# Fourteen chunks of an input projection in pairs by Strassen's method, with the weight sums on GpSimd

## The chip, the core and the metric

The kernel runs on one core of one Trainium2 chip. The metric is the device time of one execution in microseconds (us), and less is better.

## The reference

Two layers of an encoder on 256 tokens of width 2048, in float32. A layer normalises x, multiplies it by one wide matrix (`w_in`), and feeds the columns of the product to three mixers: latent attention (MLA, 8 heads), dilated attention (12 heads) and mLSTM (4 heads). Their outputs pass `w_out` and are added to x. Then comes a mixture of 16 experts, of which each token uses 2.

```python
xn = rms_norm(x, norm_mix[l])
c_q, c_kv, k_rope, dq, dk, dv, mu, mv, mo, mg = jnp.split(xn @ w_in[l], split_at, axis=-1)
...
x = x + jnp.concatenate([y_mla, y_dil, y_ml], axis=-1) @ w_out[l]
x = x + hier_moe(rms_norm(x, norm_ffn[l]), ...)
```

The change touches only `xn @ w_in[l]`, and of it the columns of dq, dk, dv, mv and mo: 3840 columns, that is 15 chunks of 256.

## The kernel before, in words

Every engine has its own program, written out by hand, and they meet at semaphores. All weights come from HBM through one queue (SyncE, the rows "SPq") into a ring of six slots of 2 MB (`ring`) and, for the experts, into three more places (XN, PR and BIAS, once their own data is no longer needed). `plan_slots` gives each load its slot, and a load is issued when the last reader of the load before it in that slot has finished. `plan_banks` gives each TensorE result its PSUM bank: `freed(name)` waits until the last result in that bank has been read, `ready(name)` until the result is there, `copied(name)` until it has been read.

A layer runs as follows. XN is x times its gain (not yet divided by its norm). First come three small chunks (c0 to c2: the latents), then the chunks mu0, mu1, mu2 of the mLSTM, with the up-projection of the latents between mu1 and mu2, and the gate rows after mu2 (`rows0`, `rows1`). During this VectorE (DVE) does the rotary embedding and the norms of the MLA queries and keys, ending with the signal `a_n`, and reads the banks of mu0 to mu2 (`keep_u`).

Then comes the stage that the change is about: chunks m0 to m14. `main(j, t)` computes 128 tokens (t is 0 or 1) by 256 columns of chunk j as 16 matmuls, one for each 128 rows of the weight: the stationary operand is a 128x128 block of XN, the moving one 128x256 of the chunk's slot. A chunk is thus 32 matmuls into one PSUM bank, two token halves side by side, and it is read from the bank once, by ScalarE (ACT, even j) or DVE (odd j), into PR, with the factor 1/norm. Chunks take banks 1 and 0 in turn, m0 bank 1.

Between the halves stand the attention steps. `MLA_AT` puts the seven steps of the MLA attention behind half 4, 6, ... 16, `DIL_AT` the nine steps of the dilated one behind halves 20 to 28, and `CONV_AT` the five taps of the mLSTM's convolution, which only DVE does, behind halves 3, 5, 7, 9 and 11. A step is a software pipeline: TensorE does the values of head pair s-3, the scores of pair s-1 and the transposes of pair s-2; DVE takes the maxima, scales the probabilities (`prob`) and reads transposes back; ScalarE does the exponentials. DVE works strictly in the order of its program.

After m14 come the output projection with the mLSTM between its parts, the router, and the experts, two at a time. GpSimd (POOL) only issues a few transfers.

Of the kernel before, what the change touches and what calls it, by code (L numbers as in the profile page):

```python
# [20 lines left out]
F32 = mybir.dt.float32  # L21
I32 = mybir.dt.int32
ALU = mybir.AluOpType
# [79 lines left out]

K_ID, K_FLIP, K_MASK = 0, P, 2 * P
# [70 lines left out]
def plan_banks():  # L175
# [17 lines left out]
    for j in range(3 * W_D // CH):  # L193
        b.once(f"m{j}", (j + 1) % 2)
        if j == 0:
            b.once("gcols", 2)
        for t in range(NT):
            if NT * j + t in MLA_AT:
                plan_attention(b, "a", H_A // 2, MLA_AT[NT * j + t])
    for j in range(3 * W_D // CH, N_SEQ):  # L200
        b.once(f"m{j}", (j + 1) % 2)
        for t in range(NT):
            at = NT * j + t - NT * (3 * W_D // CH)
            if at in DIL_AT:
                plan_attention(b, "d", H_D // 2, DIL_AT[at])
# [43 lines left out]

def plan_attention(b, k, pairs, s):  # L250
# [36 lines left out]
EXPERT_SLOTS = (IN_BIAS, 5, 0, 1, 2, 3, 4, IN_XN, IN_PR)  # L287


def plan_slots():  # L290
# [3 lines left out]
    at, held = NSLOT - 1, None  # L294
    for name in FRONT:
        if at % NSLOT == held:
            at += 1
        r.once(name, at % NSLOT)
        if name == "mw":
            held = at % NSLOT  # L300
        at += 1
    for j, name in enumerate(EXPERT):
        r.once(name, EXPERT_SLOTS[j % len(EXPERT_SLOTS)])
# [10 lines left out]
LAST_READER.update({f"B{i}": f"ob{(TILES * (i + 1) - 1) // (KT - K_A)}" for i in range(N_OUT * (KT - K_A) // TILES)})  # L314
LAST_READER.update({f"{n}{j}_{i}": f"{n}_{i}" for n in ("g0", "u0", "g1", "u1") for j in range(2) for i in range(NE // 2)})
# [19 lines left out]
def build(nc, a, consts, onehot, lncount, out):  # L335
    with ExitStack() as ctx:
# [3 lines left out]
        def sem(name):  # L340
# [37 lines left out]
            sem, ("sweep_load", "sweep_pe", "sweep_act", "sweep_dve", "sweep_own"))  # L378
        bias_dram = nc.dram_tensor("bias_dram", (H_D, 2 * S), F32).ap()
# [87 lines left out]
        par_in, small_in = sem("par_in"), sem("small_in")  # L467
        x_in, const_in, bias_in, bias_out, pos_in, rw_in, done = map(
# [16 lines left out]
        for name, n in (("sq", 4), ("sq_sum", 1), ("xg_even", KT // 2), ("xg_odd", KT // 2), ("rstd_x", 1), ("lat_std", 1), ("lat_n", 1),  # L485
# [32 lines left out]
        def empty(name, l):  # L518
# [4 lines left out]
            before = order[at - 1]  # L523
            if at > 0:
# [10 lines left out]


# [81 lines left out]
        def _(pool):  # L618
# [13 lines left out]
            for l in range(DEPTH - 1):  # L632
# [7 lines left out]
        def _(pe):  # L640
# [156 lines left out]
            for l in range(DEPTH):  # L797
# [28 lines left out]
                for t in range(NT):  # L826
                    for j in range(4):
# [9 lines left out]
                        last.then_inc(*made(name))  # L837
                project_u(2, l)
# [15 lines left out]
                for j in range(3 * W_D // CH):  # L854
                    for t in range(NT):
                        main(j, t)
                        if j == 0 and t == NT - 1:

                            pe.wait_ge(*freed("gcols", l))
                            for d in range(2):  # L860
                                pe.wait_ge(*after("rows_ready", l, d))
                                for n in range(2):
                                    for u in range(NT):
                                        c = ((n * 2 + d) * NT + u) * H_M
                                        last = mm(bank("gcols")[:, c:c + H_M], grow(d, (2, 4)[n])[:, u * P:(u + 1) * P], K[0:H_M, 0:H_M])
                            last.then_inc(*made("gcols"))
                        if NT * j + t in MLA_AT:
                            s = MLA_AT[NT * j + t]
                            if s == 0:
                                pe.wait_ge(*after("a_n", l))  # L870
                            attention("a", H_A // 2, s, l)
                for j in range(3 * W_D // CH, N_SEQ):
                    for t in range(NT):
                        main(j, t)
                        at = NT * j + t - NT * (3 * W_D // CH)
                        if at in DIL_AT:
                            if DIL_AT[at] == 0:
                                pe.wait_ge(*after("d_n", l))
                            attention("d", H_D // 2, DIL_AT[at], l)
# [4 lines left out]
                for j in range(N_OUT):  # L884
                    for q in range(2):
                        project_out("a", j, q, l)
                        if 2 * j + q in MLSTM_AT:
                            h = MLSTM_AT[2 * j + q]
                            if h == 1:
                                pe.wait_ge(*after("v_ones", l))  # L890
                                for c in range(N_SEQ - 6, N_SEQ - 3):
                                    pe.wait_ge(*copied(f"m{c}", l))
# [218 lines left out]

        qv, kv = t_h(q_mla, H_A), t_h(k_mla, H_A)
# [8 lines left out]
        def _(dve):  # L1121
# [121 lines left out]
            for l in range(DEPTH):  # L1243
# [22 lines left out]
                def keep_u(m):  # L1266
                    dve.wait_ge(*ready(f"mu{m}", l))
                    for b in range(2):
                        ins = dve.tensor_tensor(u_raw(2 * m + b), bank(f"mu{m}")[:, b * S:(b + 1) * S], rstd_b[:, 0:S], ALU.mult)
# [35 lines left out]
                keep_u(1)  # L1305
                for t in range(NT):
                    for j in (2, 3):
# [6 lines left out]
                                        src[:, :, NOPE:]).then_inc(*read(name))  # L1314

# [45 lines left out]
                for j in range(3 * W_D // CH):  # L1361
                    for t in range(NT):
                        at = NT * j + t
                        if t == NT - 1 and j % 2:
                            keep(f"m{j}", l, DQ + j * CH, CH)
                        if t == NT - 1 and j in (2, 5):
                            squares_of(j // 3)
                        if t == NT - 1 and j == 5:
                            dve.wait_ge(*after("d_std", l))
                            do(dve.reciprocal(rstd_d[:, :, :, :], std_d[:, :, :, :]))  # L1370
                            do(dve.tensor_scalar(rstd_d[:, 0, :, :], rstd_d[:, 0, :, :], HD_D ** -0.5, None, ALU.mult))
                            for n, lo in enumerate((DQ, DK)):
                                w = t_h(PR[:, :, lo:lo + W_D], H_D)
                                ins = dve.tensor_tensor(w, w, rstd_d[:, n, :, :].unsqueeze(3).to_broadcast([P, NT, H_D, HD_D]), ALU.mult)
                                if n == 0:
                                    own.did(ins)
                                else:
                                    ins.then_inc(*signal("d_n"))
                        if j == 1 and t == 0:
                            dve.wait_ge(*ready("gcols", l))  # L1380
                            dve.tensor_copy(gcol[:, :, :, :, :].rearrange("p n d t h -> p (n d t h)"), bank("gcols")[:, 0:32]).then_inc(*read("gcols"))
                        if at in MLA_AT:
                            attention("a", H_A // 2, MLA_AT[at], l)
                        if at in CONV_AT:
# [579 lines left out]
```

## Time and profile before

| | us |
|---|---|
| median of three runs (1984.39 to 1989.51) | 1985.12 |
| the profiled execution | 1986.55 |
| its span, first to last instruction | 1984.9 |
| TensorE busy in the span | 1929.6 |
| DVE / ACT / POOL busy | 472.4 / 317.6 / 5.8 |

In the rows of the profile below, PE is a TensorE matmul, "ps" is PSUM, and each float32 matmul of 256 columns appears as two records, so "x64" is 32 matmuls of the program. PEclk is the granted TensorE clock as a share of 2.4 GHz: 1.00 is the upper of its two levels, 0.50 the lower one.

### The profile page before, as it was taken

How to read it: one execution, taken by the hardware profiler on the slowest of the kernel's cores; microseconds unless marked ns; L12 is line 12 of the kernel's file. 1: busy time of each engine (PE TensorE's matmuls, PEld its weight loads, DVE VectorE, ACT ScalarE, POOL GpSimd, SP SyncE). 2: the span in 40 equal slices, each digit the busy share in tenths (PEclk: the TensorE clock that was granted, in tenths of full speed). 3: DMA queues.
4: the chain of work that ended last, by engine and by line, in shares of the span. 5: the costliest groups of instructions: out<-in, count | busy, mean ns of one | idle time of the engine just before them, and what ended most of it. 6: DMA issues, size and time to landing. Idle time of an engine off the chain costs nothing.

```text
span 1984.9 us, 26562 instructions
## 1 busy us (share of the span) xinstructions
PE 1929.6 (97%) x11730; PEld 1457.5 (73%) x11730; DVE 472.4 (24%) x1233; ACT 317.6 (16%) x831; POOL 5.8 (0%) x12
## 2 busy tenths in 40 slices
PE   6999999999899999999899999999998999999998
PEld 6788888788766666656597888877887666666665
DVE  2233313122211111221133232222222012110212
ACT  2122122210211110111021221222102111110110
POOL 0000000000000000000000000000000000000000
PEclk9999999999899999999999999999998999999999
DMA  8353333223599999999963433322346999999995
GB/s 330 137 209 127 128 127 127 92 106 149 212 414 427 428 426 427 428 427 427 413 238 146 151 116 137 130 88 88 128 157 255 426 426 427 426 428 426 428 427 242
DMA packets 39831, 538.39 MB, mean 271 GB/s; under 512 B 4665, under 2 KB 4793, under 8 KB 7201
## 3 DMA queue, kind: packets, MB, share of 16 engines
q1 hardware_dynamic: 38160, 531.46, 65.3%
q0 software_dynamic: 1296, 5.13, 0.7%
q8 instruction: 97, 1.59, 0.3%
q14 instruction: 22, 0.17, 0.0%
q10 hardware_dynamic: 256, 0.04, 0.0%
HBM read 534.49 MB, written 2.12 MB: 270 GB/s over the span
## 4 chain that ended last, share of the span: by engine, by line
PE 97%; issue 1%; DVE 1%; DMA 1%; ACT 0%; SPq 0%; DVEq 0%
PE ps L642 94%; PE ps L693 1%; DMA ring<-in_w_lat 1%; PE ps L986 0%; PE ps L709 0%; PE ps L701 0%; PE ps L907 0%; PE ps L1026 0%; ACT PR L1849 0%; PE ps L780 0%; ACT L1862 0%; SPq L562 0%; DVE v_mla L1565 0%; PE ps L820 0%; DVE prob L1607 0%
## 5 line engine op out<-in xcount | busy, mean ns | idle before, releaser
L642 PE MATMUL ps<-ring,scr 128*64 128x256 f32 (+2 forms) x3520 | 562.7, 428 | 7.1 <-issue 7.1
L642 PE MATMUL ps<-ring,XN 128*128 128x256 f32 (+2 forms) x2304 | 484.6, 371 | 17.1 <-DMA ring<-in_w_lat 17.1
L642 PEld LDWEIGHTS ps<-ring,XN 128*128 128x128 f32 x2304 | 424.5, 191 | 66.9 <-issue 19.1
L642 PEld LDWEIGHTS ps<-ring,scr 128*64 128x64 f32 (+1 forms) x3520 | 319.8, 139 | 203.9 <-issue 113.2
L642 PE MATMUL ps<-XN,ring 128*128 128x256 f32 x768 | 170.4, 381 | 0.9 <-DVE prob L1155 0.9
L642 PE MATMUL ps<-BIAS,scr 128*64 128x256 f32 (+1 forms) x608 | 159.3, 420 | 6.9 <-issue 6.9
L642 PEld LDWEIGHTS ps<-XN,ring 128*128 128x128 f32 x768 | 144.7, 190 | 26.6 <-issue 7.7
L642 PE MATMUL ps<-PR,scr 128*64 128x256 f32 (+2 forms) x576 | 158.3, 430 | 0.7 <-DVE scr L1600 0.7
L642 PE MATMUL ps<-PR,ring 128*128 128x256 f32 x640 | 142.9, 383 | 0.0
L642 PE MATMUL ps<-XN,scr 128*64 128x256 f32 (+1 forms) x576 | 141.6, 403 | 0.3 <-issue 0.2
L642 PEld LDWEIGHTS ps<-PR,ring 128*128 128x128 f32 x640 | 121.9, 192 | 19.1 <-issue 2.7
L642 PE MATMUL ps<-v_mla,PR 128*128 128x128 f32 x1024 | 122.7, 283 | 4.1 <-DVE v_mla L1565 4.1
L642 PEld LDWEIGHTS ps<-v_mla,PR 128*128 128x128 f32 x1024 | 121.2, 200 | 4.2 <-issue 4.2
L642 PE MATMUL ps<-PR,prob 128*128 128x256 f32 x512 | 118.7, 386 | 5.0 <-issue 3.8
L1589 DVE TENSOR_TENSOR v_mla<-scr,ps 128x256 f32<-128x256 f32 x32 | 13.5, 421 | 429.8 <-PE ps L642 429.8
L642 PEld LDWEIGHTS ps<-PR,prob 128*128 128x128 f32 x512 | 96.0, 192 | 24.2 <-issue 12.1
L642 PEld LDWEIGHTS ps<-BIAS,scr 128*64 128x64 f32 x608 | 83.6, 139 | 34.2 <-issue 9.9
L642 PEld LDWEIGHTS ps<-PR,scr 128*64 128x64 f32 (+1 forms) x576 | 81.2, 146 | 34.6 <-issue 24.9
L642 PEld LDWEIGHTS ps<-XN,scr 128*64 128x64 f32 x576 | 78.3, 137 | 29.4 <-issue 19.5
L1874 ACT ACTIVATE scr<-ps,par 128x128 f32<-128x128 f32 x240 | 63.8, 412 | 222.7 <-PE ps L642 222.7
L1578 DVE TENSOR_TENSOR X<-X,ps 128x512 f32<-128x512 f32 x128 | 87.9, 687 | 31.9 <-PE ps L642 31.0
L1882 ACT ACTIVATE scr<-ps 128x256 f32<-128x256 f32 x32 | 12.3, 383 | 378.7 <-PE ps L642 378.7
(231 smaller groups left out, 1009.7 us busy)
## 6 DMA issues: line engine op xcount, KB each, us to landing
ring<-in_moe_w_up SPq DMA_DIRECT2D x44, 2048.0 KB, 22.7
ring<-in_moe_w_down SPq DMA_DIRECT2D x44, 2048.0 KB, 26.5
ring<-in_moe_w_gate SPq DMA_DIRECT2D x42, 2048.0 KB, 24.5
ring<-in_w_main SPq DMA_DIRECT2D x36, 2048.0 KB, 8.1
ring<-in_w_out_a SPq DMA_DIRECT2D x10, 2048.0 KB, 8.0
PR<-in_moe_w_down SPq DMA_DIRECT2D x10, 2048.0 KB, 24.2
XN<-in_moe_w_gate SPq DMA_DIRECT2D x10, 2048.0 KB, 28.2
BIAS<-in_moe_w_up SPq DMA_DIRECT2D x10, 2048.0 KB, 23.4
```

The source lines that it names most:

```text
L642: return pe.matmul(o, lhsT, rhs, start=start, stop=stop, skip_group_check=True)
L693: last = pe.transpose(bank(name)[:, (kt * NT + t) * P:(kt * NT + t + 1) * P], prob[:, u % 2, j, t, kt * P:(kt + 1) * P], ident)
L1578: dve.tensor_tensor(x, x, bank(name), ALU.add).then_inc(*read(name))
L1589: dve.tensor_tensor(gated[:, half * CH:(half + 1) * CH], sgs[:, half * CH:(half + 1) * CH], bank(f"u{half}_{i}")[0:2 * CAP, 0:CH], ALU.mul ...
L1874: ins = act.activation(XG[:, 4 * n + k, :], bank(name)[:, k * 2 * CAP:(k + 1) * 2 * CAP], ACT.Copy, scale=pcol(l, R_FFN + 4 * n + k))
L1882: act.activation(sgs[:, half * CH:(half + 1) * CH], bank(f"g{half}_{i}")[0:2 * CAP, 0:CH], ACT.Silu).then_inc(*read(f"g{half}_{i}"))
```

## The change

Chunks m0 to m13 are taken in seven pairs. A pair is a product of a 2 by 2 block matrix (the two token halves by the two halves of the 2048 rows) with another (the two row halves by the two chunks). Instead of eight quarter products of 8 matmuls it computes seven, in the Winograd form of Strassen's method, under the names p1, p6, c11, w, p5, c21, c12. Three of them accumulate on the quarter before (`first` is False: c11 on p1, w on p6, c21 on w, c12 on p5). Chunk m14 stays as it was.

- The sums of blocks of XN (`a_sum`, four of 128x1024) are formed once a layer by DVE, in the place of x itself (the tile X). To make that possible, XN is first divided by its norm in two DVE instructions of 128x2048, between `keep_u(1)` and the reading of the up-projection. GpSimd writes X out to DRAM in the second layer (`x_dram`), and brings it back after c12 of the last pair in both.
- The sums of blocks of the weights are formed by GpSimd, four instructions of 128x2048 a pair: two into slot 3, which is held back for this (`SUMS_SLOT`), two in place.
- Every product but p1 and c11 (ACT copies) is read from its bank by DVE and added to a part of PR.
- The steps stand behind p6, w, p5 and c12 (`STEP_AFTER`); `gcols` moves from behind m0 to behind c12 of pair 0.
- Slots and banks are numbered anew. Expert loads take the slots in the order in which the front part frees them.

```diff
+PRODUCTS = ("p1", "p6", "c11", "w", "p5", "c21", "c12")
+STEP_AFTER = {"p6": 0, "w": 1, "p5": 2, "c12": 3}
...
+    for u in range(N_PAIR):
+        for name in PRODUCTS:
+            b.once(f"{name}_{u}", (u + (name in ("p6", "w", "c21"))) % 2)
...
+                pool.wait_ge(*ready("mu0", l))
+                for u in range(N_PAIR):
+                    wa, wb = w_of(2 * u), w_of(2 * u + 1)
+                    for j in (2 * u, 2 * u + 1):
+                        pool.wait_ge(*loaded(f"m{j}", l))
+                    if u:
+                        pool.wait_ge(*ready(f"p5_{u - 1}", l))
+                    own.did(pool.tensor_tensor(w_sum[:, 0], wb[:, 0:HK, :], wa[:, 0:HK, :], ALU.subtract))
+                    own.wait()
+                    pool.tensor_tensor(w_sum[:, 1], wb[:, HK:KT, :], w_sum[:, 0], ALU.subtract).then_inc(*signal("w_sums"))
+                    pool.tensor_tensor(wb[:, 0:HK, :], wb[:, HK:KT, :], wb[:, 0:HK, :], ALU.subtract).then_inc(*signal("w_sums"))
+                    pool.wait_ge(*ready(f"c11_{u}", l))
+                    pool.wait_ge(*after("w_sums", l, 3 * u))
+                    pool.tensor_tensor(wa[:, HK:KT, :], wa[:, HK:KT, :], w_sum[:, 1], ALU.subtract).then_inc(*signal("w_sums"))
...
+                def product(name, u):
...
+                    lhs, rhs, half, first = {
+                        "p1": (A[0][0], B[0][:, 0:HK], 0, True), "p6": (a_sum[:, 1], w_sum[:, 1], 0, True),
+                        "c11": (A[0][1], B[0][:, HK:KT], 0, False), "w": (a_sum[:, 2], B[1][:, 0:HK], 0, False),
+                        "p5": (a_sum[:, 0], w_sum[:, 0], 1, True), "c21": (A[1][1], B[0][:, HK:KT], 0, False),
+                        "c12": (a_sum[:, 3], B[1][:, HK:KT], 1, False)}[name]
...
+                    if name in ("p6", "w", "c21"):
+                        pe.wait_ge(*after("w_sums", l, 3 * u + ("p6", "w", "c21").index(name)))
...
+                    for k in range(HK):
+                        last = mm(bank(name)[:, half * CH:(half + 1) * CH], lhs[:, k, :], rhs[:, k, :], first and k == 0, k == HK - 1)
...
+                for h in range(2):
+                    x = XN[:, h * HK:(h + 1) * HK, :]
+                    ins = dve.tensor_tensor(x, x, rstd_b[:, 0:S].unsqueeze(1).to_broadcast([P, HK, S]), ALU.mult)
...
+                do(dve.tensor_tensor(a_sum[:, 0], quarter[1][0], quarter[1][1], ALU.add))
+                own.did(dve.tensor_tensor(a_sum[:, 1], a_sum[:, 0], quarter[0][0], ALU.subtract))
+                own.did(dve.tensor_tensor(a_sum[:, 2], quarter[0][0], quarter[1][0], ALU.subtract))
+                own.wait()
+                dve.tensor_tensor(a_sum[:, 3], quarter[0][1], a_sum[:, 1], ALU.subtract).then_inc(*signal("a_sums"))
...
+                    for lo, n, ca, cb in cells(u):
+                        to, plus = {"p6": ((0, cb), (1, ca)), "w": ((1, cb), (1, ca)), "p5": ((1, cb), (1, cb)),
+                                    "c21": ((1, ca), (1, ca)), "c12": ((0, cb), (0, cb))}[name]
+                        ins = dve.tensor_tensor(PR[:, to[0], to[1]:to[1] + n], o[:, lo:lo + n], PR[:, plus[0], plus[1]:plus[1] + n], ALU.add)
```

TensorE's program where the main stage begins, before. The rows are the end of mu2, the gate rows and chunk m0; `psum_free1` is the count of reads of bank 1.

```order
L642 MATMUL ps<-XN,ring 128x256 [waits psum_free0,slot_full5]
L642 MATMUL ps<-XN,ring 128x256 x31
L642 MATMUL ps<-K,PR 4x128 [waits psum_free6,gate_b]
L642 MATMUL ps<-K,PR 4x128 x3
L642 MATMUL ps<-K,PR 4x128 [waits psum_free7]
L642 MATMUL ps<-K,PR 4x128 x3
L642 MATMUL ps<-ring,XN 128x256 [waits psum_free1,slot_full1]
L642 MATMUL ps<-ring,XN 128x256 x31
```

The same place of the changed kernel: mu2, the gate rows, then p1, p6, c11 and w of pair 0.

```order
L704 MATMUL ps<-XN,ring 128x256 [waits psum_free0,slot_full5,xn_n]
L704 MATMUL ps<-XN,ring 128x256 x31
L704 MATMUL ps<-K,PR 4x128 [waits psum_free6,gate_b]
...
L704 MATMUL ps<-ring,XN 128x256 [waits psum_free0,slot_full2,slot_full1]
L704 MATMUL ps<-ring,XN 128x256 x7
L704 MATMUL ps<-ring,X 128x256 [waits psum_free1,a_sums,w_sums]
L704 MATMUL ps<-ring,X 128x256 x7
L704 MATMUL ps<-ring,XN 128x256 [waits psum_free0]
L704 MATMUL ps<-ring,XN 128x256 x7
L704 MATMUL ps<-ring,X 128x256 [waits psum_free1,w_sums]
```

The first product of the main stage has moved from bank 1 to bank 0, which is the bank of mu2.

DVE's program before `a_n` of the changed kernel, from the reading of the up-projection's last bank to the reading of mu2 (L1376); in the kernel before, the four rows that write X are not there and all others stand in the same order.

```order
L1429 COPY v_mla<-ps 128x256
L1437 TENSOR_TENSOR X<-XN 128x1024 [waits xn_n,dve_steps]
L1438 TENSOR_TENSOR X<-X,XN 128x1024 [waits dve_steps]
L1439 TENSOR_TENSOR X<-XN 128x1024
L1441 TENSOR_TENSOR X<-XN,X 128x1024 [waits dve_steps]
L1449 TENSOR_TENSOR scr<-PR,cs 128x256 [waits dve_steps,psum_free3,psum_free5]
...
L1461 TENSOR_TENSOR PR<-PR,rstd_a 128x2x768
L1376 COPY PR<-ps 128x256 [waits psum_full0]
```

So the reading of mu2's bank stands behind the four sums, and what follows on DVE is later by them.

GpSimd's program of the changed kernel, pairs 0 and 1 of the first layer; before, nothing stood here.

```order
L681 TENSOR_TENSOR ring<-ring 128x2048 [waits slot_full1,slot_full2,psum_full0,bias_out]
L683 TENSOR_TENSOR ring<-ring 128x2048 [waits pool_steps]
L684 TENSOR_TENSOR ring<-ring 128x2048
L687 TENSOR_TENSOR ring<-ring 128x2048 [waits w_sums,psum_full0]
L681 TENSOR_TENSOR ring<-ring 128x2048 [waits psum_full0,slot_full5,slot_full4]
```

Three sums of a pair stand in a row, and the fourth waits for c11.

## Rows read from the trace of the kernel before

**Rows 1.** The page: span, busy time by engine, and the chain that ended last.

```profile
span 1984.9 us, 26562 instructions
...
PE 1929.6 (97%) x11730; PEld 1457.5 (73%) x11730; DVE 472.4 (24%) x1233; ACT 317.6 (16%) x831; POOL 5.8 (0%) x12
...
PE 97%; issue 1%; DVE 1%; DMA 1%; ACT 0%; SPq 0%; DVEq 0%
```

**Rows 2.** Windows: the main stage of each layer, then the wait before the experts.

```profile
core 0: us, PE busy (x) PEld busy (x) DVE busy (x) ACT busy (x) POOL busy (x), PEclk, DMA share, GB/s
107.80:357.50 249.70, 249.70 (x1273) 212.51 (x1273) 71.63 (x204) 58.62 (x153) 0.00 (x0) 1.00 0.35 128
1088.80:1338.50 249.70, 249.70 (x1274) 212.51 (x1274) 71.62 (x204) 58.61 (x153) 0.00 (x0) 1.00 0.35 128
...
540.00:545.00 5.00, 5.00 (x50) 3.99 (x48) 0.00 (x0) 0.00 (x0) 0.00 (x0) 1.00 0.01 3
...
560.00:616.70 56.70, 55.67 (x445) 40.15 (x444) 5.33 (x16) 6.19 (x20) 0.00 (x0) 1.00 1.01 427
...
845.00:905.00 60.00, 58.02 (x419) 37.87 (x418) 10.60 (x23) 6.19 (x20) 0.00 (x0) 0.97 1.01 427
```

**Rows 3.** SyncE's queue in time, where the expert loads begin: start, length, transfer.

```profile
437.93 0.43 SPq L568 DMA_DIRECT2D BIAS<-in_moe_w_gate  x1
466.73 0.33 SPq L568 DMA_DIRECT2D ring<-in_moe_w_gate  x1
...
514.01 0.69 SPq L568 DMA_DIRECT2D PR<-in_moe_w_down  x1
545.54 0.33 SPq L568 DMA_DIRECT2D BIAS<-in_moe_w_down  x1
```

**Rows 4.** Groups of TensorE instructions, 246.02 to 273.9 us (m8 and m9).

```profile
L642 PE MATMUL ps<-ring,XN 128*128 128x256 f32 x128 | 27.9, 380 | 0.0
```

**Rows 5.** TensorE in time: start, length, instructions; the stage's beginning and two steps.

```profile
105.98 1.91 PE L642 MATMUL ps<-K,PR 128*4 128x128 f32 x16
107.82 14.08 PE L642 MATMUL ps<-ring,XN 128*128 128x256 f32 x64
121.83 1.94 PE L642 MATMUL ps<-K,prob 4*128 4x4 f32 x16
...
159.21 1.89 PE L642 MATMUL ps<-scr 96*128 96x256 f32 x8
160.94 1.04 PE L709 MATMUL ps<-K,PR 128*96 128x128 f32 x8
161.82 13.98 PE L642 MATMUL ps<-ring,XN 128*128 128x256 f32 x64
```

**Rows 6.** DVE in time ahead of the main stage, first layer.

```profile
81.10 0.76 DVE L1269 TENSOR_TENSOR PR<-ps,rstd_b 128x256 f32<-128x256 f32 x2 [10.50 <-PE ps L642]
85.82 0.42 DVE L1312 COPY PR<-ps 128x256 f32<-128x256 f32 x1 [3.97 <-PE ps L642]
...
92.94 1.42 DVE L1322 TENSOR_TENSOR scr<-PR,cs 128x256 f32<-128x256 f32 x4
...
102.27 0.18 DVE L1332 TENSOR_SCALAR rstd_a<-rstd_a 128x16 f32<-128x16 f32 x1
102.48 1.76 DVE L1333 TENSOR_TENSOR PR<-PR,rstd_a 128x1536 f32<-128x1536 f32 x1
104.16 1.75 DVE L1334 TENSOR_TENSOR PR<-PR,rstd_a 128x1536 f32<-128x1536 f32 x1
106.08 0.76 DVE L1269 TENSOR_TENSOR PR<-ps,rstd_b 128x256 f32<-128x256 f32 x2 [0.18 <-PE ps L642]
...
111.04 0.41 DVE L1349 SCALAR_TENSOR_TENSOR prob<-ps,neg_m 4x256 f32<-4x256 f32 x1 [4.20 <-ACT neg_m L1754]
...
117.28 0.41 DVE L1356 SCALAR_TENSOR_TENSOR prob<-prob 4x256 f32<-4x256 f32 x1
```

**Rows 7.** DVE in time near the span's start: an instruction of 128x1024, and its slowest.

```profile
19.91 1.23 DVE L1253 TENSOR_TENSOR PR<-PR 128x1024 f32<-128x1024 f32 x1 [0.51 <-ACT PR L1716]
...
35.91 1.77 DVE L1259 RECIPROCAL rstd_b<-scr 128x258 f32<-128x258 f32 x1 [10.41 <-ACT scr L1719]
```

**Rows 8.** Windows behind a pause of TensorE: the layers' border.

```profile
985.00:993.40 8.40, 4.64 (x22) 1.29 (x18) 0.69 (x1) 0.60 (x1) 0.00 (x0) 1.00 1.00 387
993.40:996.00 2.60, 2.52 (x7) 2.02 (x8) 0.63 (x1) 0.00 (x0) 0.00 (x0) 0.55 1.04 439
996.00:1000.00 4.00, 4.00 (x18) 3.46 (x17) 3.23 (x8) 1.76 (x4) 0.00 (x0) 0.86 1.01 422
```

**Rows 9.** DVE in time: an MLA step and a tap of the convolution.

```profile
177.13 1.29 DVE L1208 TENSOR_REDUCE nmx<-ps 128x2 f32<-128x512 f32 x2 [4.96 <-PE ps L642]
178.34 1.28 DVE L1221 COPY scr<-ps 128x512 f32<-128x512 f32 x2
...
179.72 0.62 DVE L1235 TENSOR_SCALAR prob<-prob,rs 128x256 f32<-128x256 f32 x2
...
180.45 0.62 DVE L1235 TENSOR_SCALAR prob<-prob,rs 128x256 f32<-128x256 f32 x2
180.98 2.45 DVE L1193 SCALAR_TENSOR_TENSOR ring<-PR,par,ring 128x255 f32<-128x255 f32 x6
```

**Rows 10.** Transfers by line: tile, queue, count, KB each, median us to landing.

```profile
ring<-in_w_main SPq DMA_DIRECT2D x36, 2048.0 KB, 8.1
...
BIAS<-bias_dram POOLq DMA_DIRECT2D x2, 2304.0 KB, 17.9
```

More of the change, by code:

```diff
@@ L293, in plan_slots @@
     r.part = "layer"
-    at, held = NSLOT - 1, None
+    order, held = [5, 0, 1, 2, 3, 4], set()
+    latest = {}
     for name in FRONT:
-        if at % NSLOT == held:
-            at += 1
-        r.once(name, at % NSLOT)
+        if name == "m0":
+            held.add(SUMS_SLOT)
+        if name == AFTER_SUMS:
+            held.remove(SUMS_SLOT)
+            order.remove(SUMS_SLOT)
+            order.insert(0, SUMS_SLOT)
+        s = next(n for n in order if n not in held)
+        order.remove(s)
+        order.append(s)
+        r.once(name, s)
+        latest[s] = name
         if name == "mw":
-            held = at % NSLOT
-        at += 1
+            held.add(s)
+    rank = {n: i for i, n in enumerate(FRONT)}
+    rank["mw"] = rank["A4"] + 0.5
+    experts = [IN_BIAS] + sorted(range(NSLOT), key=lambda n: rank[latest[n]]) + [IN_XN, IN_PR]
     for j, name in enumerate(EXPERT):
-        r.once(name, EXPERT_SLOTS[j % len(EXPERT_SLOTS)])
+        r.once(name, experts[j % len(experts)])
     return r
@@ L314 @@
 LAST_READER.update({f"B{i}": f"ob{(TILES * (i + 1) - 1) // (KT - K_A)}" for i in range(N_OUT * (KT - K_A) // TILES)})
+LAST_READER.update({f"m{j}": f"{('c21', 'c12')[j % 2]}_{j // 2}" for j in range(2 * N_PAIR)})
 LAST_READER.update({f"{n}{j}_{i}": f"{n}_{i}" for n in ("g0", "u0", "g1", "u1") for j in range(2) for i in range(NE // 2)})
@@ L855, in _ @@
+                for u in range(N_PAIR):
+                    for name in PRODUCTS:
+                        product(name, u)
+                        if name in STEP_AFTER:
+                            step(4 * u + STEP_AFTER[name])
+                for j in range(2 * N_PAIR, N_SEQ):
                     for t in range(NT):
                         main(j, t)
[L857 to L879, printed above, removed]
+                        step(NT * j + t)
@@ L890, in _ @@
                                 pe.wait_ge(*after("v_ones", l))
[L891 to L892 removed]
+                                for u in range((N_SEQ - 6) // 2, (N_SEQ - 3) // 2):
+                                    for name in ("c11", "p5", "c21", "c12"):
+                                        pe.wait_ge(*copied(f"{name}_{u}", l))
                             if h >= 1:
@@ L1359, in squares_of @@
                     dve.tensor_reduce(ss_d[:, n, :, :], t_h(PR[:, :, DV:DV + W_D], H_D), AX, ALU.add).then_inc(*signal("d_ss"))
-                for j in range(3 * W_D // CH):
-                    for t in range(NT):
[L1363 to L1384, printed above, removed]
-                            convolve(CONV_AT[at], l)
@@ L1400, in masked @@
+                for u in range(N_PAIR):
+                    for name in PRODUCTS:
+                        if name not in ("p1", "c11"):
+                            evict(name, u)
+                        if name in STEP_AFTER:
+                            step(4 * u + STEP_AFTER[name])
+                for j in range(2 * N_PAIR, N_SEQ):
+                    for t in range(NT):
+                        step(NT * j + t)
                 def masked(h):
@@ new lines, in _ @@
+                for u in range(N_PAIR):
+                    for name in PRODUCTS:
+                        if name in ("p1", "c11"):
+                            evict(name, u)
+                        if name in STEP_AFTER:
+                            step(4 * u + STEP_AFTER[name])
+                for j in range(2 * N_PAIR, N_SEQ):
+                    for t in range(NT):
+                        if t == NT - 1:
+                            act.wait_ge(*ready(f"m{j}", l))
+                            c = MO + (j - (N_SEQ - 3)) * CH
+                            act.activation(PR[:, :, c:c + CH], bank(f"m{j}").rearrange("p (t c) -> p t c", t=NT), ACT.Copy).then_inc(*read(f"m{j}"))
+                        step(NT * j + t)
@@ L1798, in _ @@
+                for name in ("c11", "p5", "c21", "c12"):
+                    act.wait_ge(*copied(f"{name}_{N_PAIR - 1}", l))
+                for j in range(2 * N_PAIR, N_SEQ):
                     act.wait_ge(*copied(f"m{j}", l))
```

228 lines of the change are left out of this document (162 added, 66 removed).

## The prediction

> **What bounds the kernel now.** I read the page first: the chain that ended last runs over TensorE for 97% of the span, and TensorE is busy for 1929.6 of 1984.9 us [rows 1]. Then the windows of the main stage: in both layers TensorE is busy for all of its 249.7 us at the upper clock, with DVE at 29%, ACT at 23% and the transfers at 0.35 [rows 2]. So here every matmul removed is time removed, as long as nobody makes TensorE wait. The experts are another matter: from 560 us on the transfers stand at 1.01 and 427 GB/s, and late pairs take 60.0 us where early ones take 56.7, so HBM bounds their end [rows 2]. The queue shows what starts that stage: loads wait for slots that TensorE frees, the last of the nine places is filled at 514, and between 540 and 545 no byte moves, until the first expert product frees BIAS at 545.5 [rows 2, 3]. The saturated stretch is thus started by TensorE, and time saved before it moves it whole.
>
> **What the change removes.** m8 and m9 have nothing between them: 128 records, 64 matmuls, in 27.9 us, 0.436 us each [rows 4]. A pair goes from 64 to 56. Seven pairs, two layers: 112 matmuls, 48.8 us. Shapes stay 128x128 by 128x256, so I use the same duration.
>
> **What it adds on DVE ahead of the stage.** Dividing XN: an instruction of 128x1536 takes 1.75 us and 128x1024 takes 1.23 [rows 6, 7], so 128x2048 takes some 2.3, two 4.5. They fit between `keep_u(1)`'s end (81.9) and the next bank at 85.8 but for 0.5, and DVE idles again before the later banks: no cost. mu2 waits for them only until 86.4 and starts later than that. The four `a_sum` instructions stand behind the last copy at 93.0 and cost 4 x 1.23, 4.9 us with their own waits. All behind them moves by 4.9: L1322 from 92.9 to 97.8, `a_n` from 105.9 to 110.8, the reading of mu2's bank from 106.1-106.8 to 110.8-111.6 [rows 6].
>
> Who waits for that? Before, m0 went into bank 1, read long ago. Now p1 of pair 0 goes into bank 0, mu2's, so it waits until 111.6, where TensorE has been free since 107.8 [rows 5]: **a new stall of 3.8 us a layer**. What such a pause does to the clock stands at the layers' border: after some 3.8 us without a matmul, 2.6 us at 0.55 and 4.0 us at 0.86 [rows 8], a loss of 2.6 x 0.45 + 4.0 x 0.14 = 1.7 us. So 5.5 a layer, 11 in all. The gate rows of DVE (111.0 to 117.7) start only 0.6 us later, and p6 of pair 0 ends at about 120, so its reading is in time [rows 6]. `gcols` moves to where its input is long ready.
>
> **What it adds while the stage runs.** A product is 8 matmuls, 3.5 us, and product n+2 needs the bank that n used: a read must end within the next product. The readings are of 128x256 from PSUM at about 0.4 us; DVE's share rises from 71.6 us by roughly 20 minus the 10 of the old readings, of 225. In an MLA step DVE is done some 4.5 us after its first maximum (177.1 to 181.0), a tap takes 2.45 [rows 9]. Behind p5 stands the step, then c21 and c12 (7 us) before p1 wants c21's bank: hidden with 3 us to spare. If that cover went, each microsecond more would show.
>
> **GpSimd.** No row has it computing, so the time T of one sum is unknown. The nearest row below is DVE's for such a shape, 2.3 us; the slowest elementwise one of the trace, 128x258 in 1.77 [rows 7], would give 14 us. I take it to be near the first, 2.3 to 5, as it is the same kind of operation. What T may be: the first two sums start when p5 of the pair before ends and p6 needs them after c21, c12 and p1, 10.5 us and the steps between. So 2T up to 10.5 costs nothing. The third has two products more, the fourth starts behind c11 and has 7 us. From T = 5.3 on there is a wait. The whole cycle: a pair will take (249.7 - 24.5 - 14) / 7 = 30.2 us on average, steps included, so 4T fits up to 7.5. The first pair is ready: m1's slot comes free with the up-projection at 92, its load lands 8.1 us later [rows 10], at 100.3, and p6 wants two sums only at about 117.
>
> The Trainium skill ("GPSIMD Engine Reference", § 3.1) measures 4497 ns for a float32 addition of 2048 elements a partition. By it 2T is 9.0, and the sum stays as it is; no run here has shown that yet.
>
> X goes out at the start of layer 2 (nobody needs its place for 80 us) and comes back after the last c12: a chunk, a step, the mLSTM's queries and the first output chunk stand between, some 29 us, and a GpSimd-queue load of 2304 KB takes 17.9 to land [rows 10]. Hidden. The new order of slots puts one expert load more ahead of the router, but all nine places were full before 545 anyway [rows 2, 3]: nothing.
>
> **The sum.** Against the profiled execution (1986.55 us, its span 1984.9 and 1.65 around it): -48.8 + 11 = -37.8, and 1 to 2 for twenty-eight more hand-overs of banks a layer: 1950. The median of the runs shown lies 1.4 below that execution, so 1948.7; I add one small delay from DVE and GpSimd sharing, and say 1950.
>
> **The rivals.**
>
> *DVE and GpSimd take turns* (this one ends on the other side). If an instruction of DVE that reads two SBUF operands, or one of the double-rate kind, cannot run while a GpSimd sum runs, and the next sum goes in front of DVE's next instruction, a group of DVE instructions is held until all three sums in a row are done, 3T after p5. For it: `prob` is scaled at 0.31 us for 256 columns, and a tap takes 0.41 [rows 9], so the former does use a double rate. Against it: nothing in the trace, for GpSimd never computed. Its price with T = 5, the largest that costs nothing by itself: ahead of the stage sums run from 100.3 to 115.3, and L1332 to L1334 of `a_n` (due at 107.2) end at 118.8, mu2's bank at 119.5: a stall of 11.7 in place of 3.8, 7.9 more. Behind p5 of pairs 1 and 2 the four scalings end at 15 + 1.5, where p1 could start at 2.9 + 7.0 = 9.9: 6.6 each. Behind p5 of pair 5 (dilated) some 4.5. With 1.7 of clock for three of these: 30.7 a layer, 61 in all, 2011 us. With T = 4 it is 3 less at each of four places: 24 less, 1987. Somewhere about 2000, then; slower once 3T is above 12.
>
> The Trainium skill speaks for this rival: "SBUF — State Buffer", § Who interferes with whom, calls the read and write port that GpSimd shares with DVE an exclusive lock, held for a whole instruction, against DVE instructions with two SBUF inputs or in a 2-port mode. It does not say who is next when both wait; if DVE keeps its turn for the group, only one sum is waited for, and this is my forecast plus some 2 to 6 us.
>
> *GpSimd is slow.* With T = 8, p6 waits 16 - 10.5 - steps: over the six changes of pair 4.6 + 2.6 + 1.6 + 3.4 + 5.5 + 0 = 17.7 a layer, 35 in all: 1985, no change. The steps of those sums are 0.9, 2.9, 3.9, 2.1, 0 and 6.6 us of TensorE after p5 and c12. With T = 6 it is 2 a layer: 1954. Above 8 slower.
>
> *The readings are late without any sharing*: every dilated step now follows the last by 3.5 to 7 us instead of 7, and DVE needs about 4.5 from scores to scaled probabilities. One microsecond in each of 15 steps would give 1980.
>
> *The saving does not arrive*, because HBM sets the experts' end: 1985. Against it stands the pause at 540 [rows 2].
>
> **How the numbers follow.** The forecast, 1940 to 1962 with sharing of one sum at most: 0.55. Taking turns: 0.28, of which a sixth still comes out faster or level. Slow GpSimd: 0.09, half of it faster. Late readings or a saving that doesn't arrive: 0.08, most of it between 1955 and 1985. The time is that of the first, 1950. To leave out no more than 2 in 10, the range reaches from 1940 (about 0.03 lie below: a stall that is smaller than thought) to 2002, which takes in T up to 8 and half of the turn-taking (0.14 lie above). The forecast's own range is 1940 to 1962. A change of 0.3% (6 us) is about what a measurement can tell here. Faster: 0.55 + 0.03 + 0.04 + 0.05 = 0.67; same 0.07; slower 0.26.
>
> **What would show it.** Right: the main stage at about 225 us with PE busy throughout, one pause of 3 to 5 us before p1 of pair 0 in each layer with clock 0.5 behind it, released by DVE's reading of mu2; sums of GpSimd started 5 us or less apart; the experts' start earlier by the same amount as the stage's end. Wrong: DVE instructions of L1299 and L1341 lasting microseconds instead of 0.3 to 0.4 (turns), PE waiting for POOL at p6 (slow sums), pauses in the dilated steps with normal DVE durations (late readings).

## The result and the profile after

The changed kernel takes 1995.01 us (median of six runs, 1993.44 to 1996.81), the kernel before 1983.68 (six runs, 1980.65 to 1989.51) on the same chip. The ratio is 1.0051, 95% interval 1.0039 to 1.0063: slower by half a per cent. The forecast was 1950 us; the rival "DVE and GpSimd take turns" had been put at about 2000.

The page of the changed kernel's profiled execution (1993.44 us), the parts that answer to [rows 1]:

```profile
span 1991.8 us, 26376 instructions
...
PE 1890.8 (95%) x11506; PEld 1421.2 (71%) x11506; DVE 596.3 (30%) x1309; ACT 316.1 (16%) x837; POOL 260.2 (13%) x71
...
PE 90%; DVE 5%; issue 3%; ACT 1%; DMA 1%; SPq 0%; DVEq 0%; ACTq 0%
```

The 224 instructions that the change takes from TensorE (112 matmuls, two records each) are gone, yet the span is 6.9 us longer. DVE, which held 1% of the chain, now holds 5%, and it is busy for 124 us more with only 76 instructions more. That is the first sign: instructions have become longer, not just more.

Windows of the first layer, in the columns of [rows 2]: the whole main stage, then its first pause and what follows it.

```profile
107.40:363.50 256.10, 234.44 (x1160) 197.09 (x1161) 127.67 (x241) 58.01 (x157) 119.26 (x28) 0.95 0.34 137
107.40:117.40 10.00, 0.06 (x1) 0.09 (x1) 9.97 (x6) 6.67 (x9) 5.84 (x2) 0.76 0.43 184
117.40:120.00 2.60, 2.60 (x6) 2.07 (x7) 2.46 (x7) 0.00 (x0) 0.00 (x0) 0.50 0.02 6
120.00:124.00 4.00, 4.00 (x13) 3.26 (x12) 2.75 (x7) 0.18 (x1) 0.00 (x0) 0.64 0.00 0
```

The stage takes 256.1 us where it took 249.7: TensorE is idle for 21.7 of them, and the granted clock is 0.95 on average. Behind the first pause it is 0.50 and 0.64 (at 0.50 it is the lower of TensorE's two levels, 1.2 GHz), a loss of 2.6 x 0.50 + 4.0 x 0.36 = 2.7 us.

TensorE in time, first layer: the rows that begin behind a pause. In brackets stands how long it was idle, and for whom.

```profile
117.34 6.44 PE L704 MATMUL ps<-ring,XN 128*128 128x256 f32 x16 [9.94 <-DVE PR L1376]
154.18 1.05 PE L771 MATMUL ps<-K,PR 128*96 128x128 f32 x8 [0.70 <-DVE gcol L1508]
180.28 5.70 PE L704 MATMUL ps<-ring,XN 128*128 128x256 f32 x16 [5.17 <-DVE PR L1501]
218.43 5.38 PE L704 MATMUL ps<-ring,XN 128*128 128x256 f32 x16 [3.57 <-DVE PR L1501]
309.51 0.63 PE L755 MATMUL ps<-K,prob 128*128 128x128 f32 x4 [2.27 <-DVE prob L1341]
```

Every pause is owed to DVE, none to GpSimd; their sum is 21.65. The second layer has the same (10.52, 0.70, 5.17, 3.57 and 2.27 us). The account of a layer: 24.4 us of matmuls removed (56 x 0.436), 21.65 of pauses and 8.4 of half-clocked matmuls added, and a rest of 0.8: +6.4. The 8.4 are 2.8, 2.1, 1.8 and 1.7 behind the four longer pauses: what the first full product behind each took to the start of the next (6.27, 5.53, 5.22 and 5.14 us) less the 3.45 of an undisturbed one.

The second stage is as long as the first (256.1 us, from 1090.55 to 1346.66), so the two lose 12.8 us. The medians differ by 11.3, the two profiled executions by only 6.9: the rest these two got back outside the stages. Of the 6.0 us by which the first stage ends later, for instance, 4.5 are left at the first expert product (542.84 against 538.38).

GpSimd in time:

```profile
99.67 4.53 POOL L681 TENSOR_TENSOR ring<-ring 128x2048 f32<-128x2048 f32 x1 [40.22 <-DMA ring<-in_w_main]
104.28 4.51 POOL L683 TENSOR_TENSOR ring<-ring 128x2048 f32<-128x2048 f32 x1
108.75 4.49 POOL L684 TENSOR_TENSOR ring<-ring 128x2048 f32<-128x2048 f32 x1
...
165.77 4.52 POOL L681 TENSOR_TENSOR ring<-ring 128x2048 f32<-128x2048 f32 x1 [2.48 <-PE ps L704]
170.37 4.52 POOL L683 TENSOR_TENSOR ring<-ring 128x2048 f32<-128x2048 f32 x1
174.85 4.54 POOL L684 TENSOR_TENSOR ring<-ring 128x2048 f32<-128x2048 f32 x1
```

DVE in the same two stretches (L1459 to L1461 and L1376 are L1332 to L1334 and L1269 of [rows 6]; L1341 is L1235 of [rows 9]):

```profile
106.58 2.24 DVE L1459 TENSOR_SCALAR rstd_a<-rstd_a 128x16 f32<-128x16 f32 x1
108.85 6.00 DVE L1460 TENSOR_TENSOR PR<-PR,rstd_a 128x1536 f32<-128x1536 f32 x1
114.78 1.75 DVE L1461 TENSOR_TENSOR PR<-PR,rstd_a 128x1536 f32<-128x1536 f32 x1
116.45 0.74 DVE L1376 COPY PR<-ps 128x256 f32<-128x256 f32 x2
...
168.91 6.13 DVE L1341 TENSOR_SCALAR prob<-prob,rs 128x256 f32<-128x256 f32 x2
174.96 0.15 DVE L1339 RECIPROCAL rs<-psum_p 128x2 f32<-128x2 f32 x1
175.15 4.65 DVE L1341 TENSOR_SCALAR prob<-prob,rs 128x256 f32<-128x256 f32 x2
179.72 0.74 DVE L1501 TENSOR_TENSOR PR<-ps,PR 128x256 f32<-128x256 f32 x2
```

Lay the two fences side by side. An instruction of 16 columns that took 0.18 us takes 2.24: it starts at 106.58 and ends at 108.82, as the second sum ends at 108.79. The next one starts at 108.85, but the third sum has started at 108.75, so it is held until 113.24 and then runs for its 1.6. The third, with no sum beside it, takes 1.75 as before. In the second stretch four scalings that took 0.31 each last 10.8 us: each sum starts less than 0.1 us behind the last, and DVE gets one instruction in between. GpSimd's own durations stay at 4.49 to 4.54. The groups of DVE by form (92 to 366 us) tell the kinds apart:

```profile
L1341 DVE TENSOR_SCALAR prob<-prob,rs 128x256 f32<-128x256 f32 x40 | 39.1, 1019 | 0.7
...
L1501 DVE TENSOR_TENSOR PR<-ps,PR 128x256 f32<-128x256 f32 x25 | 10.4, 423 | 65.5 <-PE ps L704 65.2
```

The scalings, SBUF to SBUF, average 1019 ns, the ones that met no sum included; the additions with one operand in PSUM keep 423.

### The profile page after: what moved, and what is told of

It is laid out like the page before. It is cut to its first block, busy times and chain, and to the rows that moved or that the text cites. A ratio compares the mean times of both kernels' runs of the same rounds, so it can differ in the third digit from the quotient of the medians.

```text
span 1991.8 us, 26376 instructions
## 1 busy us (share of the span) xinstructions
PE 1890.8 (95%) x11506; PEld 1421.2 (71%) x11506; DVE 596.3 (30%) x1309; ACT 316.1 (16%) x837; POOL 260.2 (13%) x71
## 4 chain that ended last, share of the span: by engine, by line
PE 90%; DVE 5%; issue 3%; ACT 1%; DMA 1%; SPq 0%; DVEq 0%; ACTq 0%
PE ps L704 88%; DVE prob L1341 2%; PE ps L755 1%; DMA ring<-in_w_lat 1%; PE ps L1077 0%; DVE rstd_a L1459 0%; PE ps L763 0%; DVE nmx L1314 0%; PE ps L771 0%; DVE ss_a L1455 0%; DVE PR L1461 0%; DVE ss_a L1456 0%; PE ps L998 0%; PE ps L1117 0%; ACT PR L1889 0%
## 5 line engine op out<-in xcount | busy, mean ns | idle before, releaser
L704 PE MATMUL ps<-ring,XN 128*128 128x256 f32 (+2 forms) x1184 | 260.6, 380 | 54.5 <-DVE PR L1376 20.5
L704 PEld LDWEIGHTS ps<-ring,XN 128*128 128x128 f32 x1184 | 223.2, 202 | 81.1 <-issue 58.0
L704 PE MATMUL ps<-ring,X 128*128 128x256 f32 x896 | 200.9, 380 | 0.0
L704 PEld LDWEIGHTS ps<-ring,X 128*128 128x128 f32 x896 | 170.4, 190 | 22.5
L1734 DVE TENSOR_TENSOR v_mla<-scr,ps 128x256 f32<-128x256 f32 x32 | 13.5, 421 | 427.5 <-PE ps L704 427.5
```

Source lines behind the costliest of these rows:

```text
L704: return pe.matmul(o, lhsT, rhs, start=start, stop=stop, skip_group_check=True)
L1734: dve.tensor_tensor(gated[:, half * CH:(half + 1) * CH], sgs[:, half * CH:(half + 1) * CH], bank(f"u{half}_{i}")[0:2 * CAP, 0:CH], ALU.mul ...
```

## The experiments

**Tiny sums.** Each sum works on 2 columns of 2048; it leaves nearly all of the sums out. All waits, banks and products stay.

```diff
-                    own.did(pool.tensor_tensor(w_sum[:, 0], wb[:, 0:HK, :], wa[:, 0:HK, :], ALU.subtract))
+                    own.did(pool.tensor_tensor(w_sum[:, 0, 0, 0:2], wb[:, 0, 0:2], wa[:, 0, 0:2], ALU.subtract))
```

> This run leaves work out: each of GpSimd's sums covers 2 columns of 2048, with every wait and signal as in the changed kernel. Taking turns (DVE instructions with two SBUF operands or at the double rate are held while a sum of 4.5 us runs): all such DVE instructions are back at 0.3 to 1.8 us, the pauses behind p5 of pairs 1, 2 and 5 are gone, the one ahead of p1 of pair 0 shrinks from 9.9 to 3.8 us, and the time falls by 2 x 24 us, from 1995 to 1946 to 1950. Late readings (DVE's added work and the short turns of the banks alone make TensorE wait): the pauses in the stage stay and the time is 1980 or more.

Measured: 1947.81 us, ratio 0.9814 (0.9795 to 0.9833). TensorE in time has one long pause left in the stage:

```profile
106.39 1.91 PE L704 MATMUL ps<-K,PR 128*4 128x128 f32 x16
111.92 6.56 PE L704 MATMUL ps<-ring,XN 128*128 128x256 f32 x16 [3.62 <-DVE PR L1376]
```

So GpSimd's work, not the schedule around it, costs 1995.0 - 1947.8 = 47 us, and what is left is the prediction's own kernel: 1948 against 1950, its pause 3.6 us against 3.8.

**Sums in parts.** The same bytes and the same arithmetic in four instructions of 512 columns, or in two of 1024 (the four with `HK // 4` shown; the other three sums are cut in the same way).

```diff
-                    own.did(pool.tensor_tensor(w_sum[:, 0], wb[:, 0:HK, :], wa[:, 0:HK, :], ALU.subtract))
+                    C = HK // 4
+                    for c in range(0, HK, C):
+                        own.did(pool.tensor_tensor(w_sum[:, 0, c:c + C], wb[:, c:c + C, :], wa[:, c:c + C, :], ALU.subtract))
```

> Each sum is four instructions of 512 columns in place of one of 2048; nothing else changes. Taking turns, one GpSimd instruction between two of DVE's: a held instruction waits at most 1.2 us, a group of four scalings is done 9 us after p5, before c21's bank is wanted at 9.9, so the pauses in the stage go and the one ahead of p1 shrinks to about 6; the time is 1950 to 1956. If a group of DVE instructions is held until GpSimd's queue has nothing ready (all three sums): the pauses stay as they are, 1990 to 1997. Late readings: no change, 1995.

> Each sum is two instructions of 1024 columns. Taking turns: a held instruction waits up to 2.3 us, four of them end 13.4 us after p5, so the pauses of 5.2 and 3.6 us become some 3.5 and 2, and the one ahead of p1 8; the time lies between the changed kernel and four pieces, 1980 to 1990. If the whole row of sums must pass: 1995.

Measured: four parts 1954.68 us, ratio 0.9852 (0.9835 to 0.9868); two parts 1980.25, ratio 0.9975 (0.9954 to 0.9996). GpSimd with four parts:

```profile
99.31 4.98 POOL L683 TENSOR_TENSOR ring<-ring 128x512 f32<-128x512 f32 x4 [39.68 <-DMA ring<-in_w_main]
104.36 6.45 POOL L686 TENSOR_TENSOR ring<-ring 128x512 f32<-128x512 f32 x4
110.77 7.29 POOL L689 TENSOR_TENSOR ring<-ring 128x512 f32<-128x512 f32 x4
```

The first sum, alone, takes 4.98 (0.45 more than whole). The second and third run beside `a_n` and take 6.45 and 7.29: now GpSimd too is held, for one instruction of DVE per part. Forty of the 47 us come back though no byte is saved; a shortage of bandwidth would not care how the columns are cut. Ahead of p1 6.2 us are left.

DVE's four scalings behind p5 of pair 1, the ones that took 10.8 us beside whole sums, with two parts and then with four:

```profile
167.35 4.10 DVE L1349 TENSOR_SCALAR prob<-prob,rs 128x256 f32<-128x256 f32 x2
171.56 4.59 DVE L1349 TENSOR_SCALAR prob<-prob,rs 128x256 f32<-128x256 f32 x2
```

```profile
164.70 2.06 DVE L1349 TENSOR_SCALAR prob<-prob,rs 128x256 f32<-128x256 f32 x2
166.87 2.51 DVE L1349 TENSOR_SCALAR prob<-prob,rs 128x256 f32<-128x256 f32 x2
```

The rows add up to 8.7 and 4.6 us. With two parts each of the four waits for one piece, of up to 2.4 us, and four such waits are little less than what whole sums cost. With four parts a piece takes 1.3 us, and the group is done before TensorE wants the bank.

**mu2 in bank 3.** One number of the plan, so that p1 of pair 0 needn't wait for DVE's late reading of mu2's bank.

```diff
-    b.once("mu2", 0)
+    b.once("mu2", 3)
```

> mu2 goes into PSUM bank 3 in place of bank 0; nothing else changes. If the pause ahead of p1 is the wait for the reading of mu2's bank: it is gone, p1 starts right behind the gate rows, but DVE is still late and reads p6 of pair 0 at 123, where w wants its bank at 118, so a pause of 5 us stands there instead: 5 us less a layer, 1983 to 1988. If p1 waited for something else (its load, the sums): 1995.

Measured: 1993.63 us, ratio to before 1.0046 (1.0033 to 1.006), so no gain over the change; 1983 to 1988 was expected. TensorE in time, then DVE:

```profile
108.71 3.72 PE L704 MATMUL ps<-ring,XN 128*128 128x256 f32 x16
...
128.69 8.88 PE L704 MATMUL ps<-ring,X 128*128 128x256 f32 x32 [9.10 <-DVE PR L1501]
```

```profile
120.00 4.70 DVE L1481 TENSOR_TENSOR_SCAN prob<-prob 4x256 f32<-4x256 f32 x1
```

p1 starts at once, and three products later w waits 9.1 us: DVE's line (`a_n`, gate rows, reading of p6) is as late as before, and the fourth sum, started earlier by the earlier c11, now falls on a scan of four rows (0.68 us without a sum beside it). The expectation had the first of these and not the second, which costs 4 us more. The pause moved, and it hardly shrank (9.94 to 9.10).

**The order of DVE.** `keep_u(2)` goes ahead of the two multiplications of `a_n`, and p6 of pair 0 is read between the gate rows of the two directions. It is combined with whole sums, four parts, eight parts and tiny sums (these leave nearly all of the sums out).

```diff
                 do(dve.tensor_scalar(rstd_a[:, 0, :, :], rstd_a[:, 0, :, :], QK_A ** -0.5, None, ALU.mult))
+                keep_u(2)
...
-                keep_u(2)
...
                 for d in range(2):
+                    if d == 1:
+                        evict("p6", 0)
                     name = f"rows{d}"
```

> Whole sums as in the change, but DVE reads mu2's bank before the two multiplications of a_n and reads p6 of pair 0 between the gate rows of the two directions. If the pause ahead of p1 is only a matter of DVE's order, p1 of pair 0 starts at about 108 instead of 117.3; the held multiplications (2.2, 6.0 and 1.75 us) then push the gate rows and the reading of p6 to about 120.5, two microseconds later than w of pair 0 wants it (118.5). That is 9.9 + 2.8 of pause and clock less and 2 more, 10.7 a layer: about 1974. The pauses of 5.2 and 3.6 us behind p5 of pairs 1 and 2 stay as they are. If the first pause is owed to the sums whatever the order, the time stays at 1995.

> The same order, and each sum in four instructions of 512 columns. Both theories of what is left in the run with four parts (1954.7, of which 6.2 us of pause and some 2.5 of clock a layer ahead of p1) are tried: if this pause is only DVE's order, it goes, and the time is 1954.7 - 2 x 8.7 = 1937; if the held group just meets the next bank that is wanted (as in the run with mu2 in bank 3, where 8.9 us came back before w), nothing is gained: 1950 or more.

> The same with eight instructions of 256 columns a sum. If what DVE loses is the length of one GpSimd instruction for each of its own, it loses half of what it does with four parts, which by now is hidden: equal to the run with four parts within 3 us, as long as a sum in eight parts stays under 7 us. If the fixed cost of a GpSimd instruction is large (a sum above 7 us), p6 or c12 begin to wait for the sums and it is slower than the one with four parts.

> The same order, and each sum on two of its 2048 columns; this leaves out nearly all of the sums, so its products are of other weights. It is the bound for whatever is done to the sums. The run with small sums in the first order gave 1947.8 with one pause of 3.6 us and some 2 of clock before p1 and 0.7 before w of pair 0 in each layer; without them about 1935. If it is above 1945, the pause moved to another place.

Measured, in the same order: 1977.52 us (ratio 0.9966, 0.9956 to 0.9977), 1939.59 (0.9775, 0.9761 to 0.9788), 1949.79 (0.9835, 0.9819 to 0.9851) and 1934.32 (0.9752, 0.9737 to 0.9767). With whole sums the pause ahead of p1 falls from 9.94 to 2.45 us and those behind p5 stay (5.17 and 3.56). What is left ahead of p1 is the scaling of 16 columns in front of `keep_u(2)`, held for 2.35 us. The expected second pause, before w, didn't come. With four parts TensorE in time shows:

```profile
108.40 3.69 PE L712 MATMUL ps<-ring,XN 128*128 128x256 f32 x16 [0.89 <-DVE PR L1384]
...
119.39 7.14 PE L712 MATMUL ps<-ring,X 128*128 128x256 f32 x32 [0.40 <-DVE PR L1485]
```

Its main stage, from the end of the gate rows to the next chunk, is 228.4 us at a granted clock of 1.00, with TensorE busy for 226.25 of them:

```profile
107.50:335.90 228.40, 226.25 (x1161) 190.90 (x1161) 119.81 (x240) 57.80 (x157) 138.09 (x107) 1.00 0.39 154
```

This is the best version of all: 2.25% faster than the kernel before, 5 us above the bound with tiny sums. Eight parts are 10 us slower than four. That expectation missed: it had a loss only for sums above 7 us, and no sum is that long by itself. GpSimd and TensorE in time of that run:

```profile
99.72 5.53 POOL L683 TENSOR_TENSOR ring<-ring 128x256 f32<-128x256 f32 x8 [39.95 <-DMA ring<-in_w_main]
105.33 9.40 POOL L686 TENSOR_TENSOR ring<-ring 128x256 f32<-128x256 f32 x8
```

```profile
114.78 5.41 PE L712 MATMUL ps<-ring,X 128*128 128x256 f32 x16 [3.39 <-POOL ring L686]
```

A sum alone takes 5.53 us in eight parts, so its fixed cost is moderate (0.14 us a part more). But the second one stands beside `a_n` and takes 9.40: between its parts DVE's long instructions get their turns, and now p6 waits for GpSimd. With 1.8 us of half clock behind this pause and a second wait for GpSimd of 0.94 us at 260.41, the stage is 233.5 us long where four parts had 228.4; in two layers that is the 10 us. Turns cut both ways.

**One long, four short.** A test of the turns themselves: the first three sums of a pair are one instruction of 1792 columns and four of 64 each. The columns are the same in all, and nearly all of the work stays in one piece. The first of the three is shown; DVE has its new order.

```diff
+                    cuts = [(slice(0, HK - 1), slice(0, CH))] + [(slice(HK - 1, HK), slice(q, q + CH // 4)) for q in range(0, CH, CH // 4)]
+                    for k, c in cuts:
+                        own.did(pool.tensor_tensor(w_sum[:, 0, k, c], wb[:, k, c], wa[:, k, c], ALU.subtract))
```

> DVE's order as in the run with whole sums and the new order (1977.5). Each of the first three sums of a pair is one instruction of 1792 columns (some 3.9 us) and four of 64 columns (0.2 to 0.3 us each), the same columns in all; the fourth stays whole. If GpSimd and DVE take turns instruction by instruction, a group of four scalings that has waited for one long instruction gets its other turns between the four short ones, and is held once instead of twice: the pauses of 5.2, 3.6 and 2.3 us behind p5 and in the dilated step fall to 1 or less, and with their clock (1.8 each) the time is about 1977.5 - 2 x (10 + 5) = 1948, between 1943 and 1958. If DVE loses by the share of time in which GpSimd computes (a matter of bandwidth or of a port shared by cycles), nothing changes: 1975 to 1981.

Measured: 1946.97 us, ratio 0.9804 (0.9791 to 0.9818); expected 1948. The pauses behind p5 are gone. GpSimd behind p5 of pair 1, and DVE's four scalings beside it:

```profile
157.89 5.25 POOL L683 TENSOR_TENSOR ring<-ring 128x1792 f32<-128x1792 f32 x5 [2.48 <-PE ps L710]
163.22 5.50 POOL L686 TENSOR_TENSOR ring<-ring 128x1792 f32<-128x1792 f32 x5
```

```profile
161.03 1.33 DVE L1347 TENSOR_SCALAR prob<-prob,rs 128x256 f32<-128x256 f32 x2
162.28 0.15 DVE L1345 RECIPROCAL rs<-psum_p 128x2 f32<-128x2 f32 x1
162.47 0.83 DVE L1347 TENSOR_SCALAR prob<-prob,rs 128x256 f32<-128x256 f32 x2
```

The group is held once, until the long instruction ends (some 4 us after 157.89, near 162), and gets the rest of its turns between the short ones: 2.2 us for four scalings where whole sums made it 10.8.

**Scalings on ACT.** DVE only forms the reciprocals and ACT multiplies; once with whole sums, once with four parts, both with DVE's new order. The line that does the work, without the signals between the two engines:

```diff
-                            ins = dve.tensor_scalar(prob[:, u % 2, j, t, :], prob[:, u % 2, j, t, :], rs[:, j, t:t + 1], None, ALU.mult)
+                                ins = act.activation(prob[:, u % 2, j, t, :], prob[:, u % 2, j, t, :], ACT.Copy, scale=rs[:, j, t:t + 1])
```

> Whole sums, new order, and ACT instead of DVE multiplies the probabilities with the reciprocals (four instructions of 128x256, about 0.4 us each, a step). If what is held is DVE alone, the multiplications take 0.4 to 0.5 us on ACT with a sum running, the pauses of 5.2, 3.6 and 2.3 us go, and the time is about 1948 (1943 to 1956). If GpSimd holds SBUF for every engine, ACT's last microseconds as DVE's did and the time stays near 1977.

> The same with sums in four parts. Against the run with four parts and DVE's scalings (1939.6; the bound with tiny sums is 1934.3) at most the 5 us to the bound are left; the scalings are hidden there already, and ACT's are longer by 0.1 us each with a hand-over more: 1938 to 1942, no difference.

Measured: 1946.03 us, ratio 0.9807 (0.9791 to 0.9824), with whole sums; 1949.41, ratio 0.9819 (0.9806 to 0.9833), with four parts. ACT with whole sums, while one sum runs from 158.14 to 162.66 and the next from 162.74 to 167.27:

```profile
161.84 1.71 ACT L1852 ACTIVATE prob<-prob,rs 128x256 f32<-128x256 f32 x4
...
178.50 1.71 ACT L1852 ACTIVATE prob<-prob,rs 128x256 f32<-128x256 f32 x4
```

Four scalings of the same shape, in and out of SBUF, take 1.71 us beside sums, and 1.71 at 178.50, when no sum runs: ACT isn't held. With four parts the expectation missed: nothing was left to win, and 10 us were lost. Two rows of TensorE that begin behind a pause name ACT, the first near an MLA step, the second in a dilated one:

```profile
216.02 3.72 PE L712 MATMUL ps<-ring,X 128*128 128x256 f32 x16 [1.59 <-ACT PR L1927]
...
274.86 1.14 PE L712 MATMUL ps<-scr 64*128 64x256 f32 x8 [1.33 <-ACT scr L1872]
```

The scalings stand ahead of ACT's copy of a product and of its reading of the transposed queries, and both come late by them. With them each stage is 2.9 us longer than with DVE's scalings, some 6 of the 10 us; the other 4 lie outside the stages and stay unexplained.

## Why the prediction was wrong

**What was removed: right.** With tiny sums the kernel is at 1947.8, with DVE's order mended as well at 1934.3, where the 1985.7 of before in that comparison less the 48.8 of the sum is 1936.9; the 2.6 us below that no row explains. The experts' start moves with the stage's end, as its step on the pause at 540 said: in that last run the first stage ends at 335.03 instead of 357.50 and the first expert product starts at 515.82 instead of 538.38, 22.5 and 22.6 us earlier. So the rival by which the saving does not arrive is out as well.

**The pause ahead of p1: right in mechanism and, without the sums, in size.** 3.62 us measured, 3.8 worked out, and 11 us for both layers with their clock; the mended order with tiny sums gives 1947.8 - 1934.3 = 13.5. The bank-3 run shows what the step left unsaid: mu2's bank was only the first to meet DVE's lateness, and without it the next one did.

**GpSimd's time: right.** T is 4.49 to 4.57 us in every sum of the changed kernel, inside the 2.3 to 5 taken and under the bound of 5.25; TensorE never waited for POOL in the changed kernel. The figure in the Trainium skill ("GPSIMD Engine Reference", § 3.1), 4497 ns, agrees.

**The failed step** is the one that priced this GpSimd time for DVE: "I add one small delay from DVE and GpSimd sharing", with its condition, "if DVE keeps its turn for the group, only one sum is waited for". The sum gave this delay 1.3 us (1948.7 to 1950); the runs with and without the sums give 47. DVE does not keep its turn: an instruction of DVE that is held gets the gap behind the running sum, and the next sum goes ahead of the instruction after it. That was the rival, priced at T = 4 and 5; half way, at 4.5, its stalls ahead of p1 and behind p5 of pairs 1, 2 and 5 are 10.2, 5.1, 5.1 and 3.0 us and the time 1999. Measured: 9.94, 5.17, 3.57 and 2.27, and 1995. Its price covered the result, and it was given 0.28.

What the runs show of the cause. That the sums do it: tiny ones give 47 us back. That the length of one instruction does it, not the work: four parts give 40 of them back, and four scalings take 10.8 us beside whole sums, 8.7 beside halves, 4.6 beside quarters and 2.2 beside one long piece with four short ones. That DVE's access is meant, not SBUF in general: ACT does the same scalings unharmed. The Trainium skill ("SBUF — State Buffer", § Who interferes with whom) calls the shared port pair an exclusive lock, held for a whole instruction, against DVE's two-input and 2-port instructions; the held and the free forms here (1019 ns for the scalings, 423 for additions with a PSUM operand) agree. Given that page and a T of 4.5, the chance of this rival should have been the larger one. What no row of before told was the order of turns.

**Slot order and the X round trip** cost nothing that shows: no wait of TensorE in the first layer's main stage names a transfer, and in layer 2 its first load is issued 26 us later (994.32 against 968.25) and still lands in time. **Late readings without sharing** did not come: with tiny sums and the new order no pause of the stage is above 0.71 us.

**Two parts against four.** That two parts recover only 15 us where four recover 40 fits the same turns, and both times were forecast from them. The pauses of the first layer add up to 21.65 us with whole sums, 15.3 with two parts (7.94, 0.71, 3.09, 3.37 and 0.21) and 7.1 with four (6.21, 0.71 and 0.17), where those behind p5 are gone with their half clock. Open is why the runs with two parts scatter over 15 us (1970.1 to 1985.3).

## What to carry to other kernels

Work given to an idle GpSimd has a price for DVE even where GpSimd itself is never waited for: count, beside each of its instructions, DVE's instructions that work from SBUF to SBUF (all but reductions and reciprocals here), and charge each up to a full GpSimd instruction, since the engines alternate. Where GpSimd must do such work, issue it in pieces about as long as DVE's own instructions (here 512 columns, 1.2 us); with pieces of 256 columns GpSimd was held so often that TensorE waited for it. And when an engine is late in order, don't move the bank that shows it, move the late engine's reading ahead of work that nobody waits for.

## What the runs showed that was not expected

- Size hardly protects an instruction: one of 16 columns (0.18 us) took 2.24 us, a scan on 4 partitions 4.70, as long as it touches SBUF in the held way; while additions of 256 columns with one operand in PSUM kept their 0.42, and a reduction of 128x1536 and a reciprocal, both from SBUF, their 1.74 and 0.35.
- The convolution's TENSOR_SCALAR, with one operand in SBUF besides its parameter columns and 0.40 us long with no sum beside it, is held too: two of the six of a tap lasted 2.14 and 4.60 us. Before, the six took 2.02:

```profile
144.88 7.95 DVE L1297 TENSOR_SCALAR ring<-PR,par 128x256 f32<-128x256 f32 x6
```

- GpSimd is held by DVE as well: a sum of 4.98 us in four parts took 7.29, and one of 5.53 in eight took 9.40, beside instructions of DVE of 1.75 us. Whole sums never showed it (4.49 to 4.57); the instruction that DVE got between two of them was a scaling of 0.31 us, which apparently fits beside the start of the next sum.
- Cutting a sum is cheap: 4.53 us whole, 4.98 in four, 5.53 in eight.
